# Gates of the last 256 sample tokens computed during the expert sums instead of in the RWKV scan

## What is computed

```python
proj = h @ lp['w_in']                                  # the last 3 * 1024 columns are pg
ya, yb, yc = hgrn2, hyena, rwkv7 of the other columns
ga, gb, gc = jnp.split(jax.nn.sigmoid(pg), N_BRANCH, axis=-1)
merged = ga * (ya @ wb[0]) + gb * (yb @ wb[1]) + gc * (yc @ wb[2])
x = x + g1 * (merged @ lp['w_out'])
h2 = rms_norm(x, lp['norm2']) * (1 + sc2) + sh2
q = (h2 @ lp['p_wq'])                                  # product keys, 16 experts for each of 8 heads
act = gelu(einsum('td,thkd->thk', h2, u_tab[expert]))
x = x + g2 * einsum('thk,thkd->td', gate * act, v_tab[expert])
```

## Time and profile before

| | us |
|---|---|
| three runs: median (lowest to highest) | 3255.39 (3243.78 to 3260.89) |
| the profiled execution, its own time | 3254.83 |
| its span | 3252.7 |
| RWKV scan, pairs 0 to 7 (769.4 to 1415) | 645.6 |
| merge of the prompt tokens (1415 to 1510) | 95.0 |
| expert stage (1510 to 3252.7) | 1742.7 |

### The profile page before, as it was taken

The page is one execution under the profiler, slowest core; times in us unless marked ns, Lnnn a source line. Parts: engine busy times, 40 slices in busy tenths (PEclk is TensorE's granted clock), DMA queues, the critical chain, the costliest instruction groups (busy, mean ns, idle before and its releaser), DMA issues.

```text
span 3252.7 us, 45370 instructions
## 1 busy us (share of the span) xinstructions
PE 2756.4 (85%) x16290; PEld 1650.2 (51%) x16290; DVE 1864.4 (57%) x3972; ACT 899.7 (28%) x2374; POOL 888.8 (27%) x812
## 2 busy tenths in 40 slices
PE   7989998898999999887888778898977777777776
PEld 5746665676666666666454334454532233222322
DVE  1029977544333333335787687786477666765454
ACT  2013332014222212122223233333223322332233
POOL 0000000000000000001443444444455555555553
PEclk9999997999999999889999899999999999999999
DMA  5113220211111111055999999999999999999997
GB/s 218 51 39 109 100 87 15 97 52 49 34 33 34 34 33 34 17 211 222 414 419 401 417 407 414 412 419 397 391 420 420 421 408 420 418 417 420 420 420 299
DMA packets 148450, 816.57 MB, mean 251 GB/s; under 512 B 16328, under 2 KB 33480, under 8 KB 62889
## 3 DMA queue, kind: packets, MB, share of 16 engines
q0 software_dynamic: 92160, 671.13, 50.1%
q1 hardware_dynamic: 56104, 142.92, 12.6%
HBM read 800.10 MB, written 13.89 MB: 250 GB/s over the span
## 4 chain that ended last, share of the span: by engine, by line
DMA 27%; PE 12%; issue 5%; DVE 4%; POOL 2%; ACT 2%; POOLq 0%; ACTq 0%; DVEq 0%; PEldq 0%
DMA pr_rows<-in_p_uv,pr_now 27%; PE pr_psy L2621 9%; DVE pr_rows L2964 3%; POOL pr_rows L2496 2%; PE pr_pss L2579 2%; ACT pr_diag L2728 1%; ACT pr_weight L2709 1%; ACT pr_act L2721 0%; DVE pr_acc L2976 0%; PE pr_pss L2552 0%; PE pr_pss L2562 0%; PE pr_pss L2599 0%; PE pr_psy L2541 0%; DVE pr_top_i L2881 0%; ACT pr_s L2698 0%
## 5 line engine op out<-in xcount | busy, mean ns | idle before, releaser
L2621 PE MATMUL pr_psy<-pr_rows,pr_diag 128*128 128x512 f32 x2432 | 1155.1, 621 | 348.1 <-ACT pr_diag L2728 304.5
L2496 POOL DMA_INDIRECT pr_rows<-in_p_uv,pr_now x640 | 793.1, 1239 | 863.5 <-PE pr_psy L2621 759.7
L2621 PEld LDWEIGHTS pr_psy<-pr_rows,pr_diag 128*128 128x128 f32 x2432 | 455.9, 196 | 1010.9 <-issue 655.9
L2964 DVE CUSTOM_DVE_ANT_0 pr_rows<-pr_rows,h_tok 128x1024 f32<-128x1024 f32 x376 | 458.5, 1225 | 319.4 <-DMA pr_rows<-in_p_uv,pr_now 316.0
L2964 DVE CUSTOM_DVE_ANT_0 pr_rows<-pr_rows,pr_h_tok 128x1024 f32<-128x1024 f32 x256 | 311.8, 1226 | 155.2 <-DMA pr_rows<-in_p_uv,pr_now 151.9
L1806 POOL TENSOR_TENSOR yT<-rw_sys,rw_bmask 128x128 f32<-128x128 f32 x40 | 18.1, 453 | 1298.9 <-DVE rw_sys L1905 1298.9
L2721 ACT ACTIVATE pr_act<-pr_dot 128x2 f32<-128x2 f32 x316 | 64.2, 203 | 1111.1 <-DVEq L2970 1110.9
L1310 PE MATMUL rw_gate_ps<-hT,rw_gate_w 128*128 128x320 f32 x768 | 269.4, 473 | 2.8 <-ACT rw_gate L1299 2.8
L2728 ACT ACTIVATE pr_diag<-con,pr_weight 128x128 f32<-128x128 f32 x632 | 216.3, 389 | 0.2
L1310 PEld LDWEIGHTS rw_gate_ps<-hT,rw_gate_w 128*128 128x128 f32 x768 | 133.3, 194 | 58.0 <-issue 16.0
L2709 ACT ACTIVATE pr_weight<-pr_gate,pr_act 128x1 f32<-128x1 f32 (+1 forms) x640 | 153.8, 287 | 22.9
(11 more groups left out here) (442 smaller groups left out, 3464.1 us busy)
## 6 DMA issues: line engine op xcount, KB each, us to landing
hg_ada_w<-in_w_ada SPq DMA_DIRECT2D x16, 1024.0 KB, 5.4
rw_gate_w<-in_w_in SPq DMA_DIRECT2D x24, 512.0 KB, 4.1
early<-in_w_branch SPq DMA_DIRECT2D x24, 512.0 KB, 11.3
pr_rows<-in_p_uv,pr_now POOLq DMA_INDIRECT x640, 12.6
st_ada_w<-in_w_ada SPq DMA_DIRECT2D x4, 2048.0 KB, 24.9
hg_w<-in_w_in SPq DMA_DIRECT2D x16, 512.0 KB, 3.6
early<-in_w_out SPq DMA_DIRECT2D x16, 512.0 KB, 8.0
early<-in_p_wq SPq DMA_DIRECT2D x16, 512.0 KB, 8.0
```

The costliest lines, as they stand in the source:

```text
L2496: nc.gpsimd.indirect_dma_start(out=rows[:, r].rearrange("p u d -> p (u d)"), out_offset=None, in_=A["p_uv"], in_offset=bass.IndirectOffset ...
L2621: last = nc.tensor.matmul(ps_y[:, c % 2, a], diag[:, r], rows[:, r, 1, a * 512:(a + 1) * 512], start=(first and r == 0), stop=False, skip_ ...
L2964: nc.vector.tensor_tensor_reduce(out=rows[:, r, 0], in0=rows[:, r, 0], in1=h_tok[c % 2], scale=1.0, scalar=0.0, op0=ALU.mult, op1=ALU.add, ...
```

## The change

In the scan a gate unit becomes one matmul with 384 tokens (the 128 prompt tokens and the first 256 sample tokens), so a tile takes 8 units and the 24 tiles have 192. PSUM tile, SBUF tile and store semaphore become double. The units before the first pair are 9, 3 and 4. In a pair five stand between the sys products, three after them (was four), one after each of D2, D4, T, W0, W1 and W2, and ten in the scan, at the points 0 and 2 alone. Pair 7 has 8 instead of 16.

The normalised input of the last 256 tokens is stored in DRAM at the end of the projections (1 MB, into unused columns of `gate_scratch`) and loaded again in the expert stage by eight DMAs of 128 KB (`h_later`).

In the expert stage the second group gets 24 new tasks `gate`, eight matmuls of 256 tokens each with 512 KB of weights from `w_in`. ACT takes each out of PSUM with the tanh that it did before from SBUF (`take_gate`). The 24 loads of stored gates of that group are gone. The plan from the end of chunk 0 to the middle of chunk 2 is laid out anew: second group's branches from (0, 25) to (1, 26) instead of from (1, 0) to (1, 17), `out` at (1, 29) on instead of (1, 19), `sums` at (2, 6) instead of (1, 28), `q` at (2, 9) instead of (1, 31), `scores` of chunk 3 at (2, 14) instead of (2, 6). DVE's selection for chunk 3 gets batches 31 to 62 of chunk 2 instead of 16 to 60, and ACT's take of those scores moves from turn 3 to turn 7.

```diff
         def gates(pe, count):
             for _ in range(count):
-                i, n = divmod(emitted[0], 2 * KD)
-                k, c = n // 2, n % 2
-                if n == 0:
+                i, k = divmod(emitted[0], KD)
+                if k == 0:
                     pe.wait_ge(gate_w_in[i % 2], 16 * (i // 2 + 1))
-                    if i:
-                        pe.wait_ge(gate_taken, i)
-                last = nc.tensor.matmul(gate_ps[:, c, 0:HALF], gate_w[:, i % 2, k],
-                                        K.hT[:, k, c * HALF:(c + 1) * HALF], start=(k == 0), stop=(k == KD - 1))
+                    if i >= 2:
+                        pe.wait_ge(gate_taken, i - 1)
+                last = nc.tensor.matmul(gate_ps[:, i % 2, 0:TRUNK], gate_w[:, i % 2, k], K.hT[:, k, 0:TRUNK],
+                                        start=(k == 0), stop=(k == KD - 1))
...
-                    sp.wait_ge(y_out, 32)
+                    sp.dma_start(A["gate_scratch"][0:KD, :, TRUNK:T].rearrange("k p t -> p k t"),
+                                 K.hT[:, :, TRUNK:T]).then_inc(y_out, 16)
+                    sp.wait_ge(y_out, 48)
...
-            AFTER_SYS = 4
-            IN_STEPS = {"D2": 2, "D4": 2, "T": 3, "W0": 2, "W1": 2, "W2": 2}
-            PER_PAIR = 3 * 2 * KD
+            AFTER_SYS = 3
+            IN_STEPS = {"D2": 1, "D4": 1, "T": 1, "W0": 1, "W1": 1, "W2": 1}
+            PER_PAIR = 3 * KD
...
             def scan_share(w, point):
-                units = IN_SCAN if w < 7 else 2 * KD
-                return units * (point + 1) // (3 * NCH) - units * point // (3 * NCH)
+                units = IN_SCAN if w < 7 else KD
+                if point % 3 == 1:
+                    return 0
+                n = 2 * (point // 3) + point % 3 // 2
+                return units * (n + 1) // (2 * NCH) - units * n // (2 * NCH)
...
+        plan("gate", BRANCHES, ((0, 24), [1] * 8))
+        plan("branch", BRANCHES, ((0, 25), [1] * 7))
         plan("tok", 2, ((1, 4), [1]))
-        plan("branch", BRANCHES, ((1, 0), [1, 2] * 6))
+        plan("gate", BRANCHES + 8, ((1, 0), [1, 1, 0] * 4))
+        plan("branch", BRANCHES + 7, ((1, 0), [1, 0, 1] * 4))
         plan("scores", 2, ((1, 12), [1]))
-        plan("branch", BRANCHES + 18, ((1, 14), [2, 1] * 2))
-        plan("out", KD, ((1, 19), [1] * KD))
-        plan("sums", 1, ((1, 28), [1]))
-        plan("q", KD, ((1, 31), [2, 2, 1, 2, 1]))
-        plan("tok", 3, ((2, 5), [1]))
-        plan("scores", 3, ((2, 6), [1]))
+        plan("gate", BRANCHES + 16, ((1, 14), [1, 0, 1, 1, 0, 1, 1, 0, 1, 1, 0, 1]))
+        plan("branch", BRANCHES + 15, ((1, 14), [1, 1, 0, 1, 1, 0, 1, 1, 0, 1, 1, 0, 1]))
+        plan("out", KD, ((1, 29), [1] * KD))
+        plan("sums", 1, ((2, 6), [1]))
+        plan("tok", 3, ((2, 9), [1]))
+        plan("q", KD, ((2, 9), [1, 2, 1, 2, 2]))
+        plan("scores", 3, ((2, 14), [1]))
...
+                    elif n == FIRST_G1:
+                        sp.wait_ge(s_mm, 2 * HEADS_P)
+                        sp.wait_ge(br_mm, BRANCHES)
+                        for k in range(KD):
+                            src = A["gate_scratch"][k][:, TRUNK:T]
+                            if k >= 4:
+                                src = src.rearrange("p (a t) -> p a t", a=2)
+                            sp.dma_start(h_later(k), src).then_inc(h_in, 16)
...
                 def task(what, i):
-                    if what == "branch":
+                    if what == "gate":
+                        n = load_of(what, i)
+                        weights(n)
+                        pe.wait_ge(h_in, 16 * KD)
+                        free((what, i))
+                        for k in range(KD):
+                            out, x = tile(what, i), h_later(k)
+                            if k >= 4:
+                                out = out.rearrange("p (a t) -> p a t", a=2)
+                            last = nc.tensor.matmul(out, w[:, n % RINGW, k], x, start=(k == 0), stop=(k == KD - 1))
+                        last.then_inc(gt_mm, 1)
...
-                           1: [(5, 0, 10), (6, 10, 22), (7, 26, 60)], 2: [(8, 16, 60)], 3: [(9, 6, 60)]}
+                           1: [(5, 0, 10), (6, 10, 22), (7, 26, 60)], 2: [(8, 31, 62)], 3: [(9, 6, 60)]}
```

More of the change, by code:

```diff
@@ L1340, in _ @@
                         pr.mm(pe, i)
-                    gates(pe, 12)
+                    gates(pe, 9)
                 @block.scalar
@@ L2409, in peer_stage @@
             task for at in sorted(TASKS) for task in TASKS[at] if task[0] != "tok"] + [("scores", 4)]
+        USES = [task for task in USERS if task[0] in ("gate", "branch", "out", "q")]
+        LOADED = [task for task in USES if task[0] != "branch" or task[1] % 2 == 0]
+        load_of = lambda what, i: LOADED.index((what, i - i % 2 if what == "branch" else i))
+        FIRST_G1 = LOADED.index(("q", 0))
         since = lambda n: n - max(m for m in range(n) if USERS[m][0] == "scores") - 1
@@ L2461, in _ @@
-                for g in range(GROUPS):
-                    for m in range(LOADS):
-                        if LOADS * g + m >= RINGW:
-                            weights(LOADS * g + m)
-                        if RINGW <= m < PAIRS:
-                            gate(BRANCHES * g + 2 * m)
-                            gate(BRANCHES * g + 2 * m + 1)
-                        elif g == 0 and m >= LOADS - RINGW:
-                            gate(BRANCHES + 2 * (m - LOADS + RINGW))
-                            gate(BRANCHES + 2 * (m - LOADS + RINGW) + 1)
+                    sp.dma_start(mg[:, i % GRING], A["gate_scratch"][i][:, tokens(0)]).then_inc(g_in[i % GRING], 16)
@@ new lines, in _ @@
+                for n in range(RINGW, len(LOADED)):
+                    weights(n)
+                    if n < PAIRS:
+                        gate(2 * n)
+                        gate(2 * n + 1)
+                    elif n == FIRST_G1:
[6 more added lines that the diff above has]
+                            sp.dma_start(h_later(k), src).then_inc(h_in, 16)
@@ L2529, in free @@
                             pe.wait_ge(s_taken, i + 1)
+                        elif what == "gate":
+                            pe.wait_ge(gated, i + 1)
                         elif what == "branch":
```

113 lines of the change are left out of this document (67 added, 46 removed).

## The result

| | median us | lowest to highest |
|---|---|---|
| before, 20 runs | 3261.27 | 3243.78 to 3270.67 |
| changed, 20 runs | 3245.22 | 3234.68 to 3250.87 |

The ratio is 0.9952, with a 95% interval of 0.9941 to 0.9963: 16 us faster. The forecast was 3215, its range 3188 to 3244. The direction was right, less than half of the gain came. The profiled execution took 3235.97 with a span of 3234.2, so span against span it is -18.5.

The account below looks back on a forecast made before the run. PE's order was taken to bound the scan and DMA bytes the expert stage. From the profiled 3254.8 us, -81.5 for the scan, +12 clock, +25 bytes and +5 PE gave -39.5, so 3215, range 3188 to 3244.

Parts of the forecast that it names:

- pairs 0 to 6 at full clock: Scan pairs: fewer gate blocks and units save 11.0 of each pair's 79.8 us, 77 us over seven pairs.
- one and a half falls at 12: Clock falls in the scan, 12 us each: 18 less the present 5.9, so +12; ends -6 and +36.
- The scan's work: Scan chunk goes from 6.58 to 5.08 us, a pair saves 11.0, without waits at S's end or R1.
- Pair 7: Pair 7's scan: five middle gate blocks removed save 3.2 to 6.1 us, taken as 4.5.
- The expert stage: Expert stage: 10.5 MB more at 420 GB/s costs +25 us, PE's added gate products +5.
- PE's 5: Expert stage: PE at 92% of DMA's time over 54 halves costs +5 us, between ends 0 and 54.
- The bound of 3 us for small transfers: Expert stage: small transfers could cost up to twice their bytes' time, moving the +25 by 3 us either way.
- The slow stretch: Expert stage: the 382 GB/s stretch, PE busy 96.4 of 100 us, stays as before, only later.
- the clock never falls: Rival: no clock falls in the new scans of pairs 0 to 6, giving 3197 us; chance 15%.
- slower through the clock: Rival: from J2 to scan's end, clock falls at 18 us each make the scan slower from five on; 3323 with seven; 5%.
- PE as the bound: Rival: PE bounds the expert sums, all 83 us of gates show instead of 30, giving 3268; chance 10%.
- units that covered waits: Rival: scan gate units covered waits of DVE, ACT and the ring; half the gain lost, about 3250; 13%.

Follow-up runs that it names:

- the other starts: Changed kernel with eight or sixteen overwritten 384-column products once ahead of pair 0, delaying all pairs 5.2 or 10.4 us: 3231.47 and 3277.13 us.
- the shifts: Eight or sixteen overwritten products ahead of pair 0: on the kernel before 3266.05 and 3278.34 us, on the changed one 3231.47 and 3277.13.
- the redistributed kernel: Changed kernel with the gate units of D2 and D4 moved behind W1 and W2, no work added: 3202.42 us, ratio to before 0.9824.
- The kernel with the late products: Changed kernel plus two overwritten 384-column products in pairs 0 to 6, one ahead of W2, one ahead of the first R1: 3200.74 us, ratio to before 0.9834.
- both other places: Changed kernel with gate units moved from D2 and D4 to W1 and W2 (late, 3202.42 us), or from W1 and W2 to D2 and D4 (early, 3221.32).

## Why the prediction was wrong

The steps of the sum against the profiled executions, in us:

| step | forecast | measured | from |
|---|---|---|---|
| pairs 0 to 6 at full clock | -77 | -72 | 560.8 to 489 |
| falls of the clock in them | +12 | +40 | 46 less 6 |
| pair 7 up to the first gather | -4.5 | -11 | 184.8 to 173.6, all in pair 7 |
| expert stage, first to last gather | +30 | +23 | 1699.9 to 1723.2 |
| ahead of the scan, after the last gather | 0 | +1 | +2.1, -1.2 |
| sum | -39.5 | -18.5 | |

**The step that failed is "one and a half falls at 12".** The mechanism was named, with its place and its price, but not its number. Five pairs fell, for 46 us, and at the other starts three for 32 and seven for 64. The price of one fall, 9.2 on average, was near the 12. With +40 in the place of +12 the sum is 3243. The profiled execution, from which the 40 is read, took 3236: pair 7 and the expert stage cost 13.5 us less than was forecast and the rest 6 more. That the result missed the range's end of 3244 by 1 us only is owed in part to these other errors, and so to luck.

Two things went wrong in reaching it. I counted one fall in seven pairs and scaled that by half, as if the changed scan had the same odds; the shifts show that the old one loses 6 to 16 us and the changed one 32 to 64 at like starts. And I wrote the reason down myself, fewer columns around the place and fewer to bring the clock back, and gave it no size. The profile before had one sign, that the scan of pair 7, with few gate columns, stayed at 1.2 GHz for 29 us. But it is a weak sign for that reason: in the changed kernel pair 7 has still fewer (8 units for 16) and its stretch is 10 us long, and in the redistributed kernel, which has the same eight, it was 10 us at one start and 31 at another.

The other terms:
- **The scan's work** was right. A chunk is 5.18 us for the forecast 5.08, the pair saves 10.2 for 11.0, nothing waits at S's end or R1.
- **Pair 7** gained more, -11. All of it lies in the pair itself, 82.0 us to 70.8; the merge behind it takes 102.8 in both. At 0.75 and 0.83 it has 41 and 24 us at the low clock. At the 0.41 us per low us that the falls of pairs 0 to 6 cost (46 us for 113) these 17 are worth 7 us, an estimate, which is what came beyond the 4.5. The forecast had no term for the clock in pair 7, so this gain was luck.
- **The expert stage** was forecast as 25 for bytes and 5 for PE. In the profiles it is 1723 to 1728 us with the new plan against 1698 to 1701 with the old, some 26 in the middle, against 25 for the bytes: nothing of PE's 5 is to be seen. (The bound of 3 us for small transfers was mis-sized, though it is not in the sum: at twice their bytes' time the eight loads cost 2.5 us more and the 24 that are gone give back 7.5 more, 5 less in all.) From 2020 to 2350 it runs at 417 GB/s with PE busy 297 of 330 us. The slow stretch moved as said: 2350 to 2450 at 384 GB/s, before 2250 to 2350 at 382.
- **The rival "the clock never falls"**, to which the Trainium skill's rule led, gave 3197 and did not happen in the changed kernel. The kernel with the late products shows that the rival's state exists: not one fall in pairs 0 to 6, and 3201. The rule itself (the Trainium skill, "TensorE: Matmul & The Clock Gate", Part 1) names how busy the engine has been, and here two kernels whose PE was busy 28.9 and 28.5 of 30 us had 0.50 and 0.94.
- **The rival "slower through the clock"** had 5%. It named the mechanism that took the gain, and seven falls were there at one start. Even so it never made the changed kernel slower than before at a like start, since a fall cost 9 us and not 18.
- **PE as the bound** and **units that covered waits** did not happen.

A forecast that held all the changed scan did here would have had +26 to +58 in the place of +12 (32 to 64 less 6): 3229 to 3261.

The one line that moves two gate units per pair from D2 and D4 to W1 and W2 makes the change worth 58 us instead of 16 (3202 against 3261), and it keeps nearly all of it when the scan begins later (57 and 54 us against the kernel before with the same shift).

## What to carry to other kernels

When a change takes wide products out of a stretch of narrow ones, PE stays busy and may still lose its clock. Look in the trace for the granted clock of each repetition, find the place where it falls, and try the wide products that remain closer to it; here both other places lost less than the even spread, and the late one nearly nothing. One profile shows one start of the stage: a scan that fell once in seven pairs may have been lucky, so delay it by 5 and 10 us and profile again before believing either a gain or a loss.

## What was not expected of the hardware

- Nine us of useless products made the kernel 44 us faster (3245.22 to 3200.74), since no pair lost its clock.
- The same scan lost 32, 46 or 64 us to the clock, depending on a start that differed by 7 to 16 us. Each number is read from one profile, and the other runs go with it but for one: the 20 runs of the changed kernel had mean clocks of 0.941 to 0.948 and times within 0.5%, five of the six shifted by 5 us had 0.951 to 0.954 (one 0.946), the seven shifted by 10 us had 0.932 to 0.938.
- A pair 7 with half the gate units had a stretch of 10 us at the low clock in its scan, where the one before had some 30.
- In pairs 0 to 6 of all these kernels, apart from a low stretch at the start of pair 0 in most of them, the clock falls in the same part, 42 to 50 us after a pair's start, from W2 to the first chunks of the scan (one short fall at 52). What ends a fall (the stretches lasted from 3.4 to 31 us over the same scan chunks) was not settled.
